# A prologue rearranged: input rows turned once, their root factors applied along the feature tiles

## The reference, cut to what matters

```python
def rmsnorm(x, w):
    y = x * rsqrt(mean(x * x, axis=-1) + EPS)
    return y * w

mod = silu(c) @ w_ada + b_ada
sh1, sc1, g1, sh2, sc2, g2 = split(mod, 6)
h = rmsnorm(x, norm_mix_w) * (1.0 + sc1) + sh1
z = h @ w_in + b_in
q_raw, f_raw, i_raw, og_raw, glu_a, glu_b, gate_a, gate_b = split(z)
...
```

## Time and profile before

| what | us |
|---|---|
| median of 3 runs | 1974.66 |
| lowest and highest of them | 1973.8, 1977.93 |
| the profiled execution, its own time | 1975.14 |
| its span in the trace | 1973.4 |

### The profile page before, as it was taken

How to read it: one execution, slowest core, us unless ns; L and a number is a source line. 1 busy time by engine, 2 the same in 40 slices (tenths; PEclk the granted TensorE clock), 3 DMA queues, 4 the chain that set the end, 5 groups by cost and what they waited for, 6 DMA issues and landing times.

```text
span 1973.4 us, 39636 instructions
## 1 busy us (share of the span) xinstructions
PE 1935.4 (98%) x16182; PEld 1876.1 (95%) x16182; DVE 1316.6 (67%) x1800; ACT 655.9 (33%) x1066; POOL 232.5 (12%) x256
## 2 busy tenths in 40 slices
PE   7999999999999999998999999999999999999998
PEld 6999999999999999988989999999999999999998
DVE  6697979786878788897775665554445544465543
ACT  6212313131413222233544433333343333433332
POOL 2300000000000000021132554700000000000000
PEclk8999999999999999999999999999999999999999
DMA  8723041413232222222366644444444544444443
GB/s 254 229 61 87 24 112 45 112 45 92 66 90 67 70 77 79 78 75 93 107 216 210 187 135 139 132 138 140 136 137 143 154 136 136 135 147 148 138 133 110
DMA packets 417245, 237.45 MB, mean 120 GB/s; under 512 B 16375, under 2 KB 411287, under 8 KB 417072
## 3 DMA queue, kind: packets, MB, share of 16 engines
q1 hardware_dynamic: 416672, 234.48, 40.6%
q10 hardware_dynamic: 416, 0.72, 0.1%
HBM read 211.91 MB, written 24.11 MB: 120 GB/s over the span
## 4 chain that ended last, share of the span: by engine, by line
PE 83%; DVE 10%; ACT 3%; issue 2%; DMA 1%; DVEq 0%; POOL 0%; ACTq 0%; SPq 0%
PE Z L887 45%; PE Z L905 27%; DVE yb L1453 4%; DVE w_lo L1305 2%; PE R L980 1%; PE Z L852 1%; PE R L924 1%; ACT w_hi L1813 1%; PE R L1006 1%; PE R L930 1%; PE R L1013 1%; PE R L1015 1%; PE R L987 1%; DVE S L1420 1%; DMA w_raw<-in_w_out_dram 1%
## 5 line engine op out<-in xcount | busy, mean ns | idle before, releaser
L1813 ACT ACTIVATE w_hi<-w_raw 128x1024 fp32r<-128x1024 f32 (+1 forms) x316 | 329.4, 1043 | 932.3 <-PE Z L887 469.7
L1305 DVE TENSOR_TENSOR w_lo<-w_raw,w_hi 128x1024 fp32r<-128x1024 f32 (+1 forms) x305 | 386.0, 1266 | 369.1 <-ACT w_hi L1813 361.4
L905 PE MATMUL Z<-h_hi,w_hi 128*128 128x352 f32 x1488 | 499.7, 336 | 2.8 <-issue 1.7
L905 PE MATMUL Z<-h_hi,w_lo 128*128 128x352 f32 x1488 | 478.4, 321 | 0.0
L905 PE MATMUL Z<-h_lo,w_hi 128*128 128x352 f32 x1488 | 477.8, 321 | 0.0
L1453 DVE SCALAR_TENSOR_TENSOR yb<-up,vec,yb 128x1024 f32 (+1 forms) x240 | 327.2, 1363 | 28.8 <-DVE yb L1453 3.7
L887 PE MATMUL Z<-h_hi,w_hi 128*128 128x352 f32 x1056 | 342.1, 324 | 0.0
L887 PE MATMUL Z<-h_hi,w_lo 128*128 128x352 f32 x1056 | 339.2, 321 | 0.0
L887 PE MATMUL Z<-h_lo,w_hi 128*128 128x352 f32 x1056 | 338.6, 321 | 0.0
L905 PEld LDWEIGHTS Z<-h_hi,w_hi 128*128 128x128 f32 x1488 | 279.5, 188 | 20.2 <-issue 16.7
L905 PEld LDWEIGHTS Z<-h_lo,w_hi 128*128 128x128 f32 x1488 | 280.3, 188 | 0.5 <-issue 0.5
(11 more groups left out here) (303 smaller groups left out, 2408.8 us busy)
## 6 DMA issues: line engine op xcount, KB each, us to landing
w_raw<-in_w_ffn_in_dram SPq DMA_DIRECT2D x132, 512.0 KB, 3.8
w_raw<-in_w_in_dram SPq DMA_DIRECT2D x64, 512.0 KB, 5.0
w_raw<-in_w_out_dram SPq DMA_DIRECT2D x48, 512.0 KB, 4.2
w_raw<-in_w_ffn_out_dram SPq DMA_DIRECT2D x48, 512.0 KB, 4.0
aw<-in_w_ada_dram SPq DMA_DIRECT2D x32, 512.0 KB, 4.0
w_raw<-in_w_ffn_out_dram SPq DMA_DIRECT2D x24, 384.0 KB, 3.4
ada_w<-in_w_ada_dram SPq DMA_DIRECT2D x16, 512.0 KB, 6.2
mbuf<-merged_scratch SPq DMA_DIRECT2D x32, 176.0 KB, 4.3
```

The source lines that it names most:

```text
L905: last = mm(out, w[:, kt, :], x[:, kt, cols], start=kt == 0 and m == 0, stop=kt == NJ - 1 and m == 2)
L1305: st.tell(V.tensor_tensor(w_lo[b.par][:, 0:n, :], w_raw[b.par][:, 0:n, :], w_hi[b.par][:, 0:n, :].bitcast(F32), ALU.subtract), w_split, b. ...
L1813: A(w_hi[b.par][:, 0:n, :], w_raw[b.par][:, 0:n, :], ACT.Copy).then_inc(w_hi_ready, 1)
```

## The change

Input rows are turned once, not twice. The root factors are not multiplied into rows; a product of the factor, spread over 128 columns, with the identity puts them as a row over the tokens on all partitions (root_row), and VectorE copies this to rsrow (copy_row). Feature tile j of the prompt is then xt times am times rsrow in one VectorE instruction (scale_prompt); ScalarE adds the shift to get h_hi; the low half is a second instruction with two tensors (prompt_low), which stands in VectorE's program behind condition and scale_prompt of the next tile. The sample columns go to GpSimd: one multiplication for all tiles, then four instructions a tile (samples), with a semaphore hs_ready for which TensorE waits too. VectorE takes the copies of turned x to xt. Row tiles have nine buffers, their loads stand ahead of all conditioning and weight loads, and these alternate (block 0, weights 0, block 1, weights 1, block 2, ...) with four conditioning buffers. The fold in a pass stands after 6 products instead of 9, the lower bounds in VectorE's program behind tiles 1 and 4, their exponentials behind tile 3 on ScalarE. There the high half of each of the first two weight blocks follows the copy of the conditioning products of the same number; on GpSimd the low half of block 1 follows the samples of tile 0.

```diff
@@ -109,11 +109,9 @@
 N_TURNS = 2 * (NC + 1)
-XN = 8
-WADA = 3
+WADA = 4
 HIST_SLOT = 2 * SLOTS
 FOLD_COL = 2 * P
-XBUF = 4
 M2 = 2 * NJ
 MBUF = 7
...
@@ -323,8 +321,9 @@
     csig = e("csig", [NSEQ, D])
     ht = e("ht", [P, NJ, NS * HIST])
     ada_w = [e(f"ada_w{i}", [P, 2, 8, P]) for i in range(WADA)]
-    xrow = [e(f"xrow{i}", [P, D]) for i in range(XBUF)]
     vrow = e("vrow", [P, 4, P])
+    rsrow = e("rsrow", [P, T])
+    xs, hs = e("xs", [P, NJ, TS]), e("hs", [P, NJ, TS])
     hbuf = (ta, tb, ysum)
...
@@ -505,13 +507,9 @@
             sp.dma_start(crow[1:NSEQ, :], c_sample).then_inc(c_loaded, 16)
             def load_x(t):
-                if t >= XBUF:
-                    sp.wait_ge(x_squared, t - XBUF + 1)
-                    sp.wait_ge(xn_scaled, t - XBUF + 1)
-                    sp.wait_ge(x_turned, 2 * (t - XBUF + 1))
                 n = P if t < NC else TS
                 src = x_prompt[0, t * P:(t + 1) * P, :] if t < NC else x_sample.rearrange("s t d -> (s t) d")
-                sp.dma_start(xrow[t % XBUF][0:n, :], src).then_inc(x_loaded[t % XBUF], 16)
+                sp.dma_start(xrow[0:n, t, :], src).then_inc(x_loaded[t], 16)
             def load_mod(j):
                 if j >= WADA:
@@ -520,7 +518,7 @@
                     sp.dma_start(ada_w[j % WADA][:, sec, :, :], wada_v[:, :, sec * D + j * P:sec * D + (j + 1) * P]) \
                         .then_inc(adaw_loaded[j % WADA], 16)
-            for t in range(XBUF):
+            for t in range(4):
                 load_x(t)
             def rows(row, tile, src):
@@ -535,17 +533,16 @@
             taps = conv_dw_w[0].rearrange("t (r c) -> (t r) c", c=P)
             for n in range(2):
                 rows(0, 2 + n, taps[n * NDW // 2:(n + 1) * NDW // 2, :])
-            load_mod(0)
-            for t in range(XBUF, NC + 1):
+            for t in range(4, NC + 1):
                 load_x(t)
             def load_first(b):
                 load_block(Idx(b), win_v[:, :, ORDER[b] * D:ORDER[b] * D + P])
-            for b in range(2):
-                load_first(b)
-            for j in range(1, NJ):
+            for j in range(NJ):
                 load_mod(j)
+                if j < 2:
+                    load_first(j)
             for b in range(2, 4):
                 load_first(b)
             old = state_conv[0].rearrange("(two s) w d -> two (s w) d", two=2)
@@ -787,29 +784,34 @@
                     col += n
                 last.then_inc(p0_done, 1)
-            def turn(t, row, normed, done, read):
-
+            def turn_tokens(t):
+
+                pe.wait_ge(x_loaded[t], 16)
                 m = tokens(t)
                 for n in range(2 * t, 2 * t + 2):
-                    wait(pe, read, n - 2)
-                    bank = turn_bank(normed, n)
+                    wait(pe, x_evac, n - 2)
+                    bank = turn_bank(n)
                     for j in range(4):
-                        last = transpose(bank[:, j * m:(j + 1) * m], row[0:m, (4 * (n % 2) + j) * P:(4 * (n % 2) + j + 1) * P],
-                                         ident[0:m, 0:m])
-                    last.then_inc(done, 1)
-
-            def turn_normed(t):
-                pe.wait_ge(xn_scaled, t + 1)
-                turn(t, xn[:, t % XN, :], 1, xn_turned, xn_evac)
+                        c = (4 * (n % 2) + j) * P
+                        last = transpose(bank[:, j * m:(j + 1) * m], xrow[0:m, t, c:c + P], ident[0:m, 0:m])
+                    last.then_inc(x_turned, 1)
+
+            def root_row(t):
+
+                m = tokens(t)
+                pe.wait_ge(rms_ready, t + 1)
+                wait(pe, row_copied, t - 2)
+                mm(row_bank(t), rs9[0:m, t:t + 1].to_broadcast([m, P]), ident[0:m, 0:m], start=True, stop=True) \
+                    .then_inc(row_made, 1)
             for t in range(NC + 1):
-                pe.wait_ge(x_loaded[t % XBUF], 16 * (t // XBUF + 1))
-                turn(t, xrow[t % XBUF], 0, x_turned, x_evac)
-                if t:
-                    turn_normed(t - 1)
+                turn_tokens(t)
+                if t >= 2:
+                    root_row(t - 2)
                 if t == 2:
                     vectors()
-            turn_normed(NC)
+            for t in range(NC - 1, NC + 1):
+                root_row(t)
             def conditioning(j):
@@ -835,7 +837,7 @@
             def first_tiles():
                 pe.wait_ge(x_evac, N_TURNS)
-                pe.wait_ge(xn_evac, N_TURNS)
+                pe.wait_ge(row_copied, NC + 1)
                 pe.wait_ge(const_ready, 3)
                 for j in range(2):
                     conditioning(j)
@@ -846,15 +848,16 @@
                     if kt == 0:
                         pe.wait_ge(w_split, 2)
                     pe.wait_ge(h_ready, kt + 1)
+                    pe.wait_ge(hs_ready, kt + 1)
                     for b in range(2):
                         for m, (w, x) in enumerate(((w_hi[b], h_hi), (w_hi[b], h_lo), (w_lo[b], h_hi))):
                             for g in range(G):
                                 last = mm(Z[b][:, g, 0:GW], w[:, kt, :], x[:, kt, g * GW:(g + 1) * GW],
                                           start=kt == 0 and m == 0, stop=kt == NJ - 1 and m == 2)
+                            if b == 0 and m == 1 and kt + 2 < NJ:
+                                fold_groups(kt + 2)
                         if kt == NJ - 1:
                             last.then_inc(block_done, 1)
-                        if b == 0 and kt + 2 < NJ:
-                            fold_groups(kt + 2)
             def hist_turn(n):
@@ -1250,27 +1253,23 @@
                 st.do(V.tensor_scalar(lbs[:, 1, :], lbs[:, 0, :], -1.0, 1.0, ALU.mult, ALU.add))
                 st.do(V.tensor_scalar(lbs[:, 2, :], lbs[:, 0, :], 1.0, None, ALU.subtract))
-            def normed_evac(t):
+            def copy_row(t):
+                dve.wait_ge(row_made, t + 1)
+                st.tell(V.tensor_copy(rsrow[:, t * P:t * P + tokens(t)], row_bank(t)), row_copied, t + 1)
+
+            for t in range(NC + 1):
                 for n in range(2 * t, 2 * t + 2):
-                    dve.wait_ge(xn_turned, n + 1)
-                    st.tell(V.tensor_copy(turned(xh, n), turn_bank(1, n)[:, 0:4 * tokens(t)].rearrange(
-                        "p (j t) -> p j t", j=4)), xn_evac, n + 1)
-
-            for t in range(NC + 1):
-                m = tokens(t)
-                dve.wait_ge(rms_ready, t + 1)
-                wait(dve, xn_turned, 2 * (t - XN + 1))
-                st.tell(V.tensor_scalar(xn[0:m, t % XN, :], xrow[t % XBUF][0:m, :], rs9[0:m, t:t + 1], None, ALU.mult),
-                        xn_scaled, t + 1)
-                if t:
-                    normed_evac(t - 1)
+                    dve.wait_ge(x_turned, n + 1)
+                    st.tell(V.tensor_copy(turned(xt, n), turn_bank(n)[:, 0:4 * tokens(t)].rearrange(
+                        "p (j t) -> p j t", j=4)), x_evac, n + 1)
+                if t >= 2:
+                    copy_row(t - 2)
                 if t == 3:
                     first_evac(1, vec[:, :], R[1][:, 0:NVEC])
-                    lower_bounds_in()
-            normed_evac(NC)
-            lower_bounds()
-
-            def modulate(j):
+            for t in range(NC - 1, NC + 1):
+                copy_row(t)
+
+            def condition(j):
                 def add_bias(sec):
                     return V.tensor_scalar(mod[:, sec * NJ + j, :], R[j % 2][:, FOLD_COL + sec * 16:FOLD_COL + sec * 16 + NSEQ],
@@ -1282,20 +1281,32 @@
                 st.settle()
                 st.tell(V.tensor_scalar(am[:, j, :], mod[:, SC1 * NJ + j, :], ones[:, :], vec[:, V_MIX + j:V_MIX + j + 1],
                                         ALU.add, ALU.mult), am_ready, j + 1)
+
+            def scale_prompt(j):
                 st.settle()
-                buf = hbuf[j % 3]
-                st.do(V.tensor_scalar(buf[:, 0:TP], xh[:, j, 0:TP], am[:, j, 0:1], mod[:, SH1 * NJ + j, 0:1],
-                                      ALU.mult, ALU.add))
-                s = seqs(buf[:, TP:T])
-                st.do(V.tensor_tensor(s, seqs(xh[:, j, TP:T]), per_seq(am[:, j, 1:NSEQ]), ALU.mult))
-                st.settle()
-                st.tell(V.tensor_tensor(s, s, per_seq(mod[:, SH1 * NJ + j, 1:NSEQ]), ALU.add), h_full, j + 1)
+                st.tell(V.scalar_tensor_tensor(hbuf[j % 3][:, 0:TP], xt[:, j, 0:TP], am[:, j, 0:1], rsrow[:, 0:TP],
+                                               ALU.mult, ALU.mult), h_full, j + 1)
+
+            def prompt_low(j):
+
                 dve.wait_ge(h_hi_ready, j + 1)
-                st.tell(V.tensor_tensor(h_lo[:, j, :], buf[:, 0:T], h_hi[:, j, :].bitcast(F32), ALU.subtract), h_ready,
-                        j + 1)
-
-            for j in range(NJ):
-                modulate(j)
+                st.tell(V.scalar_tensor_tensor(h_lo[:, j, 0:TP], hbuf[j % 3][:, 0:TP], mod[:, SH1 * NJ + j, 0:1],
```

(81 more changed lines are left out.)

14 lines of the change are left out of this document (8 added, 6 removed).

## The result

The changed kernel took **1979.91 us** in the median of 21 runs (1976.59 to 1981.92). The kernel before took 1976.75 beside it (21 runs, 1972.08 to 1978.07). The ratio is 1.0017, with a 95% interval of 1.0011 to 1.0023. Repeated it was 1.0011 (1.0002 to 1.0020). The change costs 2 to 3 us. The forecast was no change, 1974.8, and a range that ended at 1979.5. The three runs of before that it was made on are the first of these 21, and their median, 1974.66, lies 2.1 us under that of all 21; so 2.1 us of the 5.1 between forecast and result are the base. One of the 12 runs of a kernel further down (tile by tile with memsets, again) took 2695.03 us at a granted clock of 0.653; its ratio leaves this run out, and the median of the other eleven is 1974.55 where 1974.61 is given.

What follows compares the result with a forecast made beforehand. TensorE, busy 98% of the span, was taken as the bound. Start 35.7 plus passes 32.2 plus 7.06 put the next output tile at 75.0 against 74.84, so 1974.8 us, no change; range 1968.5 to 1979.5.

Steps and rivals of the forecast that it cites:

- Transfers: Prologue loads: input done at 15.4, then 2.62 MB in 8.8 us; conditioning block 1 lands at 25.7, block 2 at 31.0.
- lag: Prologue loads: a block lands 1.5 us after its bytes (0.5 to 2.2), counted as -1.0 to +0.7 in the range.
- The start S: Start of TensorE's first product in the prologue: 35.7, which is 5.0 us before the old 40.67.
- The lock: Prologue: VectorE's first two-input scaling waits for GpSimd's whole low half of weight block 1, 29.15 to 31.5.
- The passes: Feature-tile passes after the first: 5.12 us each against TensorE's 4.56, so the passes lose 5.1 us to tile 6.
- The loop through VectorE: In the passes: products 1.05, fold to bias 0.54, to scaling 0.73, pair 2.5, hand-over 0.05, sample 0.25; 5.12 us.
- The first pass: First feature-tile pass at the low clock: products 2.0, fold 1.06, then 0.73 + 2.5 + 0.3, making 6.6 us.
- The sample operation's 0.25: In each pass, one of GpSimd's four small sample instructions delays VectorE by 0.25 us; bounds zero and 1.0.
- Rival 3: Passes and start: all four GpSimd sample operations go ahead of VectorE's pair, 5.0 us slower, 1979.8; chance 0.13.
- The mark: Start of the next output tile behind the passes: 75.0 in place of 74.84, leaving the kernel where it was.
- The step that failed: Behind the prologue: queue order is unchanged, so the total changes by as much as the next output tile's start.
- The prediction's own test: Whole kernel: next output tile's start and total moving by different amounts would refute that nothing behind it reacts.

Runs made afterwards that it cites:

- tile by tile with memsets, again: Changed kernel with each feature tile's condition, scaling and low half done whole, plus 17 one-column VectorE memsets, rerun on another chip: 1974.61 us, 0.9988 against the kernel before.
- taking it apart: Changed kernel with VectorE making a tile's low half right behind that tile's scaling, start left alone: 1978.04 us, 1.0007 against the kernel before.
- with and without memsets: Changed kernel plus 17 one-column memsets of an unused tile on VectorE ahead of the heads' loop: 1978.87 us, 1.0012 against the kernel before.
- idle turns: Changed kernel plus 22 unread identity turns on TensorE behind each of the first two folds: 1977.11 us; with the 17 VectorE memsets too, 1976.23; both 1.0002.
- the tile-by-tile order: Changed kernel with VectorE doing condition, scaling and low half of each tile whole from tile 0: 1976.80 us, 1.0000; with 17 VectorE memsets 1974.23, 0.9990.

## Why the prediction was wrong

Point by point, with its own steps:

- **Transfers.** Block 1 at 25.7 was forecast, 27.38 measured; block 2 at 31.0 and 32.68. Both are 1.7 late, and each term of the sum has a part. The 4.6 MB of input and vectors had moved by 16.0 us, not 15.4: the sag to 191 GB/s behind the vector rows wasn't in the sum, which took the middle of its two rates. The 2.62 MB behind them went at 283 GB/s, not 298: 9.3 us in place of 8.8. And the block landed 2.1 us behind its bytes, not 1.5. They lie inside the bounds that the prediction gave (transfers +1.4, lag +0.7), and all go the same way. (The rate of the 512-byte rows was nearly right, 283 to 290 GB/s; the Trainium skill's rule of "DMA: Bandwidth & Descriptors", section Specifications, by which they would run at line rate, does not agree with them.)
- **The start S.** 35.7 forecast, 37.24 measured: the 1.7 of the transfer carried through, less 0.2. The lock was there as forecast, but it held the small scale factor, not the scaling; the price was nearly the same.
- **The passes.** 5.12 forecast, 4.96 measured. The loop through VectorE is what sets the pace, and taking it apart gave 4.57. The first pass, 6.6 forecast and 6.26 measured, has another reason than the forecast's: TensorE goes from it into the second without a wait, since the low half of tile 1 is done at 43.32 and TensorE's own work, at half the clock to 41.1, ends at 43.50. The sample operation's 0.25 was the part that failed: it measured 0 to 0.1, since VectorE's pair left GpSimd no turn. Rival 3 falls by the same rows.
- **The mark.** 75.0 forecast, 75.48 measured: the late start and the shorter passes nearly cancel. Its change against before was 0.64 in the profiled pair, and about 1.3 with each side's second profile taken in (1.02 over the two of the changed kernel, -0.3 over before's). The spread is mostly that of the first pass, 6.26 and 7.06, by how long the clock stays at 0.50: to 41.1 and to 42.8.
- **The step that failed** is "I take the change of the 74.84 mark as the change of the time, because behind it the order of every queue is as before". The order is as before, and the time still changed, for two reasons. VectorE's program had lost 17 instructions, and with that a stop of 0.35 us came up in each of three rounds at a place where TensorE waits in the end, 1.1 us together; whether it stood elsewhere in the kernel before, where it cost nothing, the traces do not show. And the profile that served as base had lost nothing in the output projection, where all others lost 0.4 to 4.0. The prediction's own test, that a mark and a total moved by different amounts would refute this step, is what came out: 0.64 and 5.1.
- **The base.** Three runs of before gave 1974.66, later groups 1976.4 to 1976.8. That is 2 us of the miss and no hardware at all.

So the changed kernel's 2 to 3 us are, by these runs, about 1.3 in the prologue and 1.1 from the stop. In the prologue, over two profiles of each kernel, the start wins 3.0, and the first pass loses 1.1 and the next five 3.1. The rest is within what one profile differs from another. That the forecast of the mark came within 0.5 is in part luck: a start 1.5 too early and passes 1.1 too long. The 1.1 is shown in the traces; that it also stands in the median is not shown on the changed kernel itself: of the comparisons with and without memsets the one on the changed kernel gives -0.4 to 1.0 us, that with idle turns 0.9, that in the tile-by-tile order 2.2 to 2.6, each uncertain by about 2. The last is larger than the stop; why is open. So is what the stop is: no run here tells whether it is the loading of instructions or something else. Another number of memsets, which would move it once more, was not tried.

What the change could have won is shown by the tile-by-tile order. It takes the start's gain without the loop's loss, and with the memsets it stands 2 us under the kernel before.

## What to carry to other kernels

When one engine's work for the next tile is put ahead of what the current tile still lacks, write the loop out through every engine and compare it with the bound engine's pass: here it made 4.56 into 4.96 and ate an earlier start of 3.4 us. An earlier start on an engine that has just waited is worth less than it looks, since it runs on the low clock. And where differences of a few us in 2000 are at stake, neither one profile nor three runs are a base: take a second profile of the same kernel and see how far it moves against the first.
